# The start of a two-layer diffusion block on one core: parameter and weight-slot transfers moved, squares summed by TensorE, head units in four parts

## The reference

```python
def rmsnorm(x, g):
    x32 = x.astype(jnp.float32)
    y = x32 * lax.rsqrt(jnp.mean(x32 * x32, axis=-1, keepdims=True) + EPS)
    return (y * g.astype(jnp.float32)).astype(x.dtype)
...
    sc = jax.nn.silu(c)
    scc = jax.nn.silu(c_ctx)[None, :]
...
        m = jnp.split((sc @ w_ada[l] + b_ada[l])[:, None, :], N_MOD, axis=-1)
...
        h = h + 0.5 * m[2] * swiglu(modulate(rmsnorm(h, ffn1_norm_g[l]), m[0], m[1]),
                                    ffn1_w_in[l], ffn1_w_out[l])
```

## Time and profile before

| | |
|---|---|
| median of 3 runs | 1584.08 us (1582.62 to 1589.05) |
| the profiled execution | 1582.28 us, its span 1580.4 us |
| PE busy | 1559.6 us, 99% of the span, 9010 matmul records |
| DVE busy | 1003.7 us, 64% |
| ACT busy | 627.1 us, 40% |
| POOL busy | 81.3 us, 5% |
| transfers | 249.94 MB, mean 158 GB/s, 364 GB/s in the first of 40 slices |

### The profile page before, as it was taken

How to read it: one execution, slowest core, us unless ns; L and a number is a source line. 1 busy time by engine, 2 the same in 40 slices (tenths; PEclk the granted TensorE clock), 3 DMA queues, 4 the chain that set the end, 5 groups by cost and what they waited for, 6 DMA issues and landing times.

```text
span 1580.4 us, 22218 instructions
## 1 busy us (share of the span) xinstructions
PE 1559.6 (99%) x9010; PEld 1335.5 (85%) x9010; DVE 1003.7 (64%) x1245; ACT 627.1 (40%) x848; POOL 81.3 (5%) x102
## 2 busy tenths in 40 slices
PE   8999999999999999999999999999999999999997
PEld 5888888888988888888888898888888897999997
DVE  6777773773967577777363267777455268965554
ACT  4433322232784343333232252333232249654553
POOL 0000000011100200000000100000001110000001
PEclk9999999999999999999999999999999999999999
DMA  9565553653322255555363336555355323456563
GB/s 364 199 192 182 184 163 120 206 194 94 116 76 76 94 172 188 184 188 174 106 200 100 100 120 212 191 183 197 97 167 153 107 80 122 154 167 197 190 207 110
DMA packets 72297, 249.94 MB, mean 158 GB/s; under 512 B 11664, under 2 KB 12816, under 8 KB 71184
## 3 DMA queue, kind: packets, MB, share of 16 engines
q1 hardware_dynamic: 72208, 248.70, 48.1%
HBM read 247.62 MB, written 1.05 MB: 157 GB/s over the span
## 4 chain that ended last, share of the span: by engine, by line
PE 94%; ACT 2%; DVE 1%; issue 1%; DMA 1%; SPq 0%; POOL 0%; DVEq 0%; POOLq 0%; ACTq 0%
PE bank L425 84%; PE bank L544 2%; PE bank L550 2%; PE bank L546 2%; DMA ada_head<-head_w 1%; PE bank L440 1%; PE bank L706 1%; PE bank L677 1%; PE bank L679 1%; PE bank L678 1%; PE bank L708 0%; PE bank L506 0%; PE bank L456 0%; ACT w_hi L831 0%; DVE w_lo L1116 0%
## 5 line engine op out<-in xcount | busy, mean ns | idle before, releaser
L831 ACT ACTIVATE w_hi<-raw 128x1024 fp32r<-128x1024 f32 x317 | 335.8, 1060 | 812.5 <-PE bank L425 795.3
L1116 DVE TENSOR_TENSOR w_lo<-raw,w_hi 128x1024 fp32r<-128x1024 f32 x317 | 387.7, 1224 | 372.8 <-ACT w_hi L831 372.5
L425 PE MATMUL bank<-z_hi,w_hi 128*128 128x512 f32 (+1 forms) x1480 | 536.1, 362 | 0.4 <-DVE scr L1310 0.4
L425 PE MATMUL bank<-z_lo,w_hi 128*128 128x512 f32 (+1 forms) x1480 | 532.6, 360 | 0.0
L425 PE MATMUL bank<-z_hi,w_lo 128*128 128x512 f32 (+1 forms) x1480 | 532.4, 360 | 0.0
L425 PEld LDWEIGHTS bank<-z_hi,w_hi 128*128 128x128 f32 x1480 | 278.2, 188 | 46.5 <-issue 3.2
L425 PEld LDWEIGHTS bank<-z_lo,w_hi 128*128 128x128 f32 x1480 | 278.2, 188 | 42.5 <-issue 1.0
L425 PEld LDWEIGHTS bank<-z_hi,w_lo 128*128 128x128 f32 x1480 | 278.1, 188 | 42.6
L425 PE MATMUL bank<-h_hi,w_hi 128*128 128x512 f32 (+1 forms) x770 | 266.7, 346 | 0.0
L425 PE MATMUL bank<-h_lo,w_hi 128*128 128x512 f32 (+1 forms) x770 | 266.0, 345 | 0.0
L425 PE MATMUL bank<-h_hi,w_lo 128*128 128x512 f32 (+1 forms) x770 | 265.9, 345 | 0.0
(11 more groups left out here) (167 smaller groups left out, 1220.6 us busy)
## 6 DMA issues: line engine op xcount, KB each, us to landing
raw<-weights SPq DMA_DIRECT2D x320, 512.0 KB, 4.0
ada_raw<-ada_w SPq DMA_DIRECT2D x128, 512.0 KB, 4.3
ada_head<-head_w SPq DMA_DIRECT2D x8, 1024.0 KB, 18.2
res<-x_t SPq DMA_DIRECT2D x4, 512.0 KB, 5.3
ada_raw<-gate_w SPq DMA_DIRECT2D x4, 256.0 KB, 5.3
out<-res SPq DMA_DIRECT2D x4, 256.0 KB, 3.1
ws<-sgu_w SPq DMA_DIRECT2D x2, 256.0 KB, 4.2
bs<-sgu_b SPq DMA_DIRECT2D x2, 256.0 KB, 4.3
```

What stands on the lines that cost most here:

```text
L425: m = pe.matmul(bank[:, to], w, x[:, k, at], start=start and i == 0, stop=stop and i == 2, skip_group_check=True)
L831: act.activation(w_hi[:, r, :], raw[:, r, :], ACT.Copy).then_inc(hi_ready, 1)
L1116: dve.tensor_tensor(w_lo[:, r, :], raw[:, r, :], w_hi[:, r, :].bitcast(F32), ALU.subtract).then_inc(lo_ready, 1)
```

## The change

Four things change, all in the first norm and the first three slots.

- **Transfers.** The parameters go behind all of x; slot 0 goes behind head 0, slot 1 behind head 1, slot 2 behind head 2, slot 3 behind head 7. ACT's and DVE's splits of slots 0 to 3 move accordingly.
- **Sums.** Rows 0 to 3 of the squares no longer go through DVE's additions: PE sums each directly (`first_sums`, 16 more one-column matmuls), and DVE adds only rows 4 to 7 (3 additions for 7).
- **Power.** POOL takes one power over both streams, once both are scaled.
- **Head units.** Units 4 to 7 are cut into four parts of 8 matmuls; parts 0, 1 and 2+3 stand before the three products of a step. In the first steps the order of units and products changes too.

```diff
@@ -366,13 +368,11 @@
                 sp.dma_start(res[:, rows, :], x_t[:, rows, :]).then_inc(x_in[i], 16)
-                if i == 1:
-                    sp.dma_start(par[:], params).then_inc(par_in, 16)
-            slot_dma(0, 0)
+            sp.dma_start(par[:], params).then_inc(par_in, 16)
             for k in range(KD):
                 sp.dma_start(ada_head[:, k, :], head_w[k]).then_inc(head_in[k], 16)
-                if k in (0, 1, 5):
-                    q = {0: 1, 1: 2, 5: 3}[k]
+                if k in (0, 1, 2, 7):
+                    q = min(k, RING - 1)
                     slot_dma(q, q)
@@ -466,9 +466,8 @@
                 if n == 0:
-                    pe.wait_ge(const_ready, 1)
-                    pe.wait_ge(head_sum, KD - 1)
-                    sums(ss_bank(n, s), 2, s, True, True).then_inc(ss_done, 1)
+                    pe.wait_ge(head_sum, KD - 1 - SUMS_DIRECT)
+                    sums(ss_bank(n, s), 2, s, False, True).then_inc(ss_done, 1)
                     return
@@ -481,6 +480,15 @@
+            def first_sums(d):
+
+                pe.wait_ge(sq_ready, d + 1)
+                for s in range(2):
+                    for j in range(2):
+                        m = 2 * s + j
+                        pe.matmul(ss_bank(0, s)[:, j:j + 1], head_sq[:, d, m * P:(m + 1) * P], ones[:, 0:1],
+                                  start=d == 0 and j == 0, stop=False, skip_group_check=True)
+
@@ -521,13 +536,26 @@
-                    for step in range(KD + len(banks) - 1):
-                        if HEAD_AHEAD <= step < KD - 1:
-                            head_unit(step + 1)
-                        for q in range(len(banks) - 1, 0, -1):
-                            swept(step - q, q)
-                        if step < HEAD_AHEAD:
-                            head_unit(step + 1)
-                        swept(step, 0)
+                    head_unit(1)
+                    swept(0, 0)
+                    head_unit(2)
+                    swept(0, 1)
+                    swept(1, 0)
+                    swept(1, 1)
+                    head_unit(3)
+                    swept(0, 2)
+                    swept(2, 0)
+                    for step in range(HEAD_WHOLE, KD + len(banks) - 1):
+                        more = step < KD - 1
+                        if more:
+                            head_part(step + 1, 0)
+                        swept(step - 2, 2)
+                        if more:
+                            head_part(step + 1, 1)
+                        swept(step - 1, 1)
+                        if more:
+                            head_part(step + 1, 2)
+                            head_part(step + 1, 3)
+                        swept(step, 0)
                     return
@@ -805,6 +833,8 @@
             pe.wait_ge(const_ready, 1)
             throwaway(WARM_UP, p_ada, T)
+            for d in range(SUMS_DIRECT):
+                first_sums(d)
             norm_sums(0, 0)
             norm_sums(0, 1)
@@ -1082,12 +1112,10 @@
-                if d == 3:
-                    act.wait_ge(par_in, 16)
-                    act.activation(c_cols[:, :, 0:2], par[:, C_CVEC:C_CVEC + 2 * KD].rearrange("p (k s) -> p k s", s=2),
-                                   ACT.Silu).then_inc(cvec_ready, 1)
+            act.wait_ge(par_in, 16)
+            act.activation(c_cols[:, :, 0:2], par[:, C_CVEC:C_CVEC + 2 * KD].rearrange("p (k s) -> p k s", s=2),
+                           ACT.Silu).then_inc(cvec_ready, 1)
             split_hi(0, 0)
-            split_hi(1, 1)
             norm(0, 0)
@@ -1180,8 +1209,6 @@
                     total(0)
-                if n == 0:
-                    split_lo(0, 0)
                 variance(0)
@@ -1243,8 +1270,8 @@
                             z_low(k, s)
-                        if k in (0, 1, 7):
-                            q = {0: 1, 1: 2, 7: 3}[k]
+                        if k in (0, 1, 2, 7):
+                            q = min(k, RING - 1)
                             split_lo(q, q)
@@ -1638,6 +1665,11 @@
+                if n == 0:
+
+                    pool.wait_ge(var_ready, 2)
+                    pool.tensor_tensor(tokr[:], tok[:], mhalf[:], ALU.pow).then_inc(rstd_ready, 2)
+                    return
```

More of the change, by code:

```diff
@@ L53 @@
 WARM_UP = 8
-HEAD_AHEAD = 3
+HEAD_WHOLE = 3
+HEAD_PARTS = 4
+SUMS_DIRECT = 4
 ADA_RING = 2
@@ L496, in norm, with head_part @@
                     throwaway(6, pa[SIDE])
[L498 to L502, removed]
+            def head_part(b, part):
+                if part == 0:
+                    if b >= 2:
+                        pe.wait_ge(head_turned, b - 1)
+                    pe.wait_ge(head_in[b], 16)
                 w = ada_head[:, b, :].rearrange("p (k m j i) -> p k m j i", k=KD, m=2, j=4)
-                for k in range(KD):
+                for k in range(part * KD // HEAD_PARTS, (part + 1) * KD // HEAD_PARTS):
                     for j in range(4):
@@ L507, in head_unit @@
                                       start=(k == 0), stop=(k == KD - 1), tile_position=(0, 32 * j))
-                m.then_inc(head_mm, 1)
+                if part == HEAD_PARTS - 1:
+                    m.then_inc(head_mm, 1)
+            def head_unit(b):
+                for part in range(HEAD_PARTS):
+                    head_part(b, part)
             def first_slots(n, base, banks):
@@ L876, in norm @@
                         if n == 0 and s == 1:
-                            for q in {0: (2,), 6: (3,)}.get(k, ()):
+                            for q in {0: (1,), 1: (2,), 6: (3,)}.get(k, ()):
                                 split_hi(q, q)
@@ L1152, in norm @@
                 if n == 0:
-                    for d in range(1, KD):
+                    first = SUMS_DIRECT
+                    for d in range(first + 1, KD):
                         dve.wait_ge(sq_ready, d + 1)
-                        if d > 1:
-                            dve.wait_ge(head_sum, d - 1)
-                        dve.tensor_tensor(scr[:, 2, :], head_sq[:, 0, :] if d == 1 else scr[:, 2, :], head_sq[:, d, :],
+                        if d > first + 1:
+                            dve.wait_ge(head_sum, d - first - 1)
+                        dve.tensor_tensor(scr[:, 2, :], head_sq[:, first, :] if d == first + 1 else scr[:, 2, :], head_sq[:, d, :],
                                           ALU.add).then_inc(head_sum, 1)
```

## The result

The changed kernel takes 1590.57 us (median of 20 runs, 1587.05 to 1597.91), the kernel before 1584.91 us (20 runs, 1582.61 to 1590.46). The ratio is 1.0035, 95% interval 1.0024 to 1.0046: 5.7 us longer, less than 0.5%. The profiled execution took 1590.09 us, its span is 1588.2 us (1580.4 before).

A forecast was written before the change was run, and what follows sets the result against it. PE, busy 99% of the span, bounds the kernel, so lateness in the start passes to the end. 2.9 + 3.0 - 1.05 + 0.55 = +5.4 us on 1584.1 gives 1589.5 us; range 1584 to 1595 for 8 in 10.

The forecast's parts named there:

- first scaling: DVE's first scaling in the first norm, behind sums, power and spread: from 15.22 to 18.4 us, 3.2 later.
- unit 4: Start of head unit 4 on PE, behind DVE's rows and slot splits: 30.5 us for 27.56, +2.9.
- eight more visits to the strips: Units 4 to 7 on PE get two more visits each, about 0.37 us beside their own work: +3.0 us.
- second instruction stall: PE out of instructions in unit 4: 1.34 us shrinks to between 0 and 0.6, taken as 0.5; -1.05.
- row 7: PE's wait for the last row's `z_lo` before swept(7, 0), unit 7 ending one product before step 6 is over: +0.55.
- swept(7, 0): Product on PE after the wait for the last row; PE continuous from there, 5.4 us later than before.
- Direct sums: 32 one-column records on PE behind the throwaway matmuls, 3.5 us; the DVE additions saved are worth 0.05 us.
- One power: POOL takes one power instead of two that took 1.40 us: 0.7 us, the greater width costed at nothing.
- Transfers: Heads 0, 1 and 2 land earlier; both PE waits, 2.6 us, go, but only because PE comes later.
- rival (c): Granted clock falls to 0.50 in PE's start: +5 in all, 1594.5 us; slower by over 0.5%; chance 15%.
- (a): Direct sums run beside throwaway matmuls, strips cost nothing extra, heads land sooner, both stalls go: -3.7, 1580.4 us; chance 8%.
- (b): Start late as summed, but short visits to the strips cost at most half: +1 to +3.9, say 1587; chance 10%.

The follow-up runs named there:

- e7: Changed kernel with whole head units and 4 throwaway matmuls for 8; median 1583.16 us, kernel before 1584.14.
- e2: Kernel before with the direct sums alone (16 more one-column matmuls, 4 fewer DVE additions); median 1586.59 us, kernel before 1584.52.
- e9: Changed kernel without direct sums, with whole head units, 4 wide and 16 narrow throwaway matmuls for 8 wide; median 1582.83 us, kernel before 1584.32.
- e4: Changed kernel with head units 4 to 7 whole again; median 1587.36 us, kernel before 1584.52.
- e5: Kernel before with head units 4 to 7 cut into four parts, nothing else; median 1586.15 us, kernel before 1584.14.
- e6: Changed kernel without direct sums and with whole head units; median 1584.46 us, kernel before 1584.14.
- e1: Kernel before with 12 throwaway matmuls for 8, nothing else; median 1585.40 us, kernel before 1584.52.
- e3: Changed kernel with the direct sums taken back (all 7 additions on DVE); median 1587.53 us, kernel before 1584.52.
- e8: Kernel before with the last 4 throwaway matmuls of 512 columns replaced by 16 of 128; median 1582.71 us, kernel before 1584.14.
- run 1404: Not a follow-up run: the program's last loops execute 1404 matmuls of 256 columns, 159.42 us in the profile of the kernel before.

## Why the prediction came out

The forecast was 1589.5 us, +5.4; measured are 1590.57 and +5.7, in the range and on the side that was said. Its two large terms are borne out by the experiments, its clock is not, and part of the closeness is luck. By its steps, in the profile (before to after):

| step | predicted | measured |
|---|---|---|
| first scaling | +3.2 | +5.7 (15.22 to 20.94) |
| unit 4 | +2.9 | +5.6 (27.56 to 33.17) |
| eight more visits to the strips | +3.0 | +2.8 (3.99 for 3.29, four times) |
| second instruction stall | -1.05 | -1.55 (unit 4 took 2.58 us for 1.03; none left) |
| row 7 | +0.55 | +0.56 |
| swept(7, 0) | +5.4 | +7.4 (43.57 to 50.97) |

- **Direct sums: the mechanism was right.** PE had no room in front of them, and e7 shows that place, not number, makes the cost. As an edit alone they cost 2.1 us by the median (e2), with an interval that includes nothing, and 2.5 to 2.7 in the changed kernel.
- **One power** was mis-sized: 1.04 us for width 4, not 0.7. From the first sum to the first scaling, e9 with one power takes 3.21 us, the kernel before with two 3.14: it costs as much as it saves. In the changed kernel it is off the path: the power ends at 19.2, and the spread waits for head unit 0 until 19.61.
- **Visits to the strips: right to 0.2 us.** 0.35 us each (2.8 / 8). e4 and e5 show the same steps without and with the parts (3.30 and 3.98 us). The Trainium skill (TensorEngine Tiling, Key Properties) says that changing the tiling mode drains the engine; the price of a visit agrees with that, and that the engine drains no run here shows by itself.
- **Transfers:** both waits for heads went, as said, only because PE came later. e6 shows that without that lateness their gain is eaten by a longer stall.
- **The step that failed is the clock**, rival (c), given 15%: it fell in the profile, which the prediction itself had named as a sign of being wrong. The first scaling is 2.5 us later than forecast (20.94 for 18.4), and all of it lies in records at half clock: the sums end 1.3 us later, unit 0 takes 0.7 more, the spread up to the first scaling 0.5. The second stretch at 0.50 cost next to nothing, because DVE sets the pace there: from the first scaling to unit 4 the forecast was 12.1 us, measured are 12.23. The stall, which went wholly, gave 0.5 back. That makes +7.4 at swept(7, 0), and 7.8 in the span, for 5.4. The fall had been priced at +5; its own items (2.2, 0.9, 0.9 and 9 to 20 products of 0.2) come to 5.8 to 8.0, and it does not say what takes the rest off; the profile shows 2.5.
- **Why the median is nearer than the profile.** Of the 20 timed runs of the changed kernel, leaving out the 6 that lie 6 us higher for the reason of the last section, 5 have a mean granted clock of 0.996 over the span and take 1587.05 to 1587.97, and 9 have 0.993 or 0.994 and take 1590.09 to 1591.68, 2.6 us more. Against the 14 corresponding runs of before (median 1584.0) that is +3.9 and +6.5. The forecast, made for a clock that stays up, lies between the two: it is too high for the first group and leaves out what lowers the second, and that these two errors nearly cancel in the median is luck. In which stretch a timed run lost its clock is not shown: the mean also holds a late norm, in which the eleven profiles have 3.4 or 6.8 us at 0.50, and the end. And the kernel before is not free of it, though its profile shows no fall in the start: of its 87 runs beside the experiments (66 without the 6 us), 37 have 0.996 or 0.997, median 1583.2, and 29 have 0.993 to 0.995, median 1584.5.
- **Rivals (a) and (b) fell.** All 32 direct records run behind the throwaway matmuls, and a short visit costs as much as a long one. The lower end of the range, 1584, was called that of (b), which by its +1 would be 1585; nothing hangs on it.
- **What lets the clock fall.** With direct sums it fell within the sum records (changed, e2) or 0.8 to 1.0 us behind them in head unit 0 (e4, e7), and in none of the seven others (before, e1, e3, e5, e6, e8, e9) at that place; e1 shows about the same lateness by dense matmuls without a fall. That the one-column records are the cause there is therefore supported, by eleven profiles, one of each kernel; it is not shown by a run that changes only their kind. But e3, e5 and e6 fell at an instruction stall of 1.94, 1.44 and 2.54 us, while before (1.16 and 1.34), e1 (1.26) and e8 (0.59) did not, nor did e2 behind its stall of 1.69. So a stall of that size does not decide it alone. The second fall of the changed kernel came behind a wait of 1.74 us for DVE, and e4 waited 1.60 us at the same place without one. The Trainium skill (TensorE: Matmul & The Clock Gate, Part 1) names idleness as the cause; the falls of e3, e5 and e6 agree, while in the four kernels with direct sums PE is busy without a gap up to the first fall.

Open: why some executions of the same kernel, the kernel before included, lose more clock than others. It was not tried to hold the clock up inside the direct sums by dense matmuls between them.

## What to carry to other kernels

Work moved onto an engine is cheap only at a place in its queue where nothing urgent stands behind it. PE had 2.6 us of waits for transfers, but they come after the first scaling, and the sums are needed before it; so 3.5 us of one-column sums, queued behind a warm-up that had been sized to end just in time, delayed everything. In place of half of the warm-up (e7) they did not. Before cutting a group of matmuls in another tile shape into parts, count the changes of shape: here 0.35 us each, whatever the part holds. And where an engine runs short instructions under full transfer queues, an "issue" gap may be the end of an instruction block, which a different number of records ahead of it moves or shrinks.

## What was not expected of the hardware

The last loops of the program run 1404 matmuls of 256 columns. The chain of waits of the kernel before and of e1 (one row each):

```profile
1401.69 159.42 PE bank L425 x1404
```

```profile
1403.96 165.64 PE bank L425 x1404
```

The pitch is 0.1135 us in one and 0.1180 in the other, at a granted clock of 1.00 in both, which makes 6.2 us. Of the nine other profiles two, e2 and e5, have the slow pitch (165.64), the rest 159.42 or 159.43. It does not follow the edits: e2 has it and the changed kernel, which has the same direct sums, has not. The three profiled executions with the slow pitch (1591.12, 1594.64 and 1594.19 us) are among the high runs of their kernels and the other eight among the low ones, so I take it for the 6 us by which 6 of the 20 runs of before and 6 of the 20 of the changed kernel lie above the rest. What chooses the pitch in an execution stays open.
